# GpSimd's weight sums of the third pair of projection blocks, placed ahead of the wait for the last tokens' rows

## What is computed

```python
def token_mixers(h, p, s_gdn, conv_buf, s_rwkv, h_prev):
    proj = h @ p['w_in']
    qa, ka, va, za, ba, aa, ub, vb = split_cols(proj[..., :C_OFF], AB_SPLITS)
    qkv, new_conv = causal_short_conv(jnp.concatenate([qa, ka, va], axis=-1), conv_buf, p['gdn_conv_w'])
    ...                                   # gated DeltaNet on q, k, v
    u = jax.nn.gelu(ub.astype(f32), approximate=False)
    ...                                   # vs: normalised gelu(vb)
    o_b = u * sgu_mix(vs, p['sgu_w'], p['sgu_b']).reshape(b, L, D_B)
    ...                                   # RWKV-7 on the remaining columns
    mix = jnp.concatenate([o_a, o_b, o_c], axis=-1).astype(h.dtype) @ p['w_out']
    return mix, new_gdn, new_conv, new_rwkv, h[:, -1], vs.reshape(b, L, D_B)
```

## Time and profile before

| | us |
|---|---|
| time before, median of 3 runs | 1267.41 (1266.54 to 1269.93) |
| time of the profiled execution | 1270.75 |
| its span, first to last instruction | 1269.0 |
| TensorE busy | 1188.6 (94% of the span) |
| VectorE busy | 518.8 (41%) |
| ScalarE busy | 339.5 (27%) |
| GpSimd busy | 560.3 (44%) |

### The profile page before, as it was taken

How to read it: one execution, slowest core, us unless ns; L and a number is a source line. 1 busy time by engine, 2 the same in 40 slices (tenths; PEclk the granted TensorE clock), 3 DMA queues, 4 the chain that set the end, 5 groups by cost and what they waited for, 6 DMA issues and landing times. The chain is left out here.

```text
span 1269.0 us, 31522 instructions
## 1 busy us (share of the span) xinstructions
PE 1188.6 (94%) x12736; PEld 849.9 (67%) x12736; DVE 518.8 (41%) x1252; ACT 339.5 (27%) x787; POOL 560.3 (44%) x818
## 2 busy tenths in 40 slices
PE   9996999999999999999998999959999999999990
PEld 7785888856666667778764554447777777777760
DVE  3453887755285524564532113252222222222223
ACT  5002003253342145456432132211111111111114
POOL 7403111020650236878732021026666666666662
PEclk9998999999999999999998999969999999999995
DMA  6301120114303100000084313189999897898838
GB/s 208 100 1 34 35 67 18 32 60 137 63 21 92 50 17 15 17 23 16 11 243 159 101 67 113 45 303 381 308 373 338 270 374 247 289 374 288 266 51 290
DMA packets 139882, 187.12 MB, mean 147 GB/s; under 512 B 37272, under 2 KB 85903, under 8 KB 139786
## 3 DMA queue, kind: packets, MB, share of 16 engines
q1 hardware_dynamic: 123018, 164.87, 38.3%
q0 software_dynamic: 15936, 20.57, 7.8%
q10 hardware_dynamic: 832, 0.33, 0.1%
HBM read 156.41 MB, written 29.32 MB: 146 GB/s over the span
## 5 line engine op out<-in xcount | busy, mean ns | idle before, releaser
L527 PE MATMUL ps<-hT,w_in 128*128 128x352 f32 (+1 forms) x624 | 190.1, 464 | 1.8 <-ACT cb L806 1.2
L527 PEld LDWEIGHTS ps<-hT,w_in 128*128 128x128 f32 x624 | 118.0, 191 | 69.3 <-issue 4.6
L3041 POOL DMA_INDIRECT sum_rows<-slot_out,scatter_rows x76 | 121.9, 1604 | 38.2 <-POOL scatter_rows L3040 25.7
L3173 DVE TENSOR_TENSOR slot_T<-slot_raw_T,vecs 128x256 f32<-128x256 f32 x75 | 32.5, 434 | 208.5 <-PE ps L3086 207.6
L3086 PE MATMUL ps<-qkv,slot_T 128*32 128x256 f32 x1920 | 109.9, 379 | 3.1 <-DVE slot_T L3173 1.6
L3086 PEld LDWEIGHTS ps<-qkv,slot_T 128*32 128x32 f32 x1920 | 74.8, 110 | 32.3 <-DVE slot_T L3173 4.2
L3018 POOL DMA_INDIRECT gathered<-h_rows,gather_rows x79 | 83.5, 1057 | 19.6 <-issue 12.2
L3130 ACT ACTIVATE slot_silu<-ps 128x128 f32<-128x128 f32 x77 | 21.4, 278 | 225.0 <-PE ps L3086 222.8
L3086 PE MATMUL ps<-cb,slot_T 128*32 128x256 f32 x1408 | 80.6, 379 | 0.0
L3086 PEld LDWEIGHTS ps<-cb,slot_T 128*32 128x32 f32 x1408 | 55.4, 110 | 20.5
L3136 ACT ACTIVATE slot_out<-ps,slot_weights 128x256 f32<-128x256 f32 x76 | 36.2, 476 | 112.2 <-PE ps L3097 112.2
(11 more groups left out here) (748 smaller groups left out, 2405.0 us busy)
## 6 DMA issues: line engine op xcount, KB each, us to landing
qkv<-in_expert_w_gate SPq DMA_DIRECT2D x6, 2048.0 KB
qkv<-in_expert_w_up SPq DMA_DIRECT2D x6, 2048.0 KB
qkv<-in_expert_w_down SPq DMA_DIRECT2D x6, 2048.0 KB
cb<-in_expert_w_gate SPq DMA_DIRECT2D x5, 2048.0 KB
cb<-in_expert_w_up SPq DMA_DIRECT2D x5, 2048.0 KB
zg<-in_expert_w_down SPq DMA_DIRECT2D x5, 2048.0 KB, 21.8
third_w_down<-in_expert_w_down SPq DMA_DIRECT2D x5, 2048.0 KB, 17.0
w_in<-in_w_in SPq DMA_DIRECT2D x18, 512.0 KB, 4.7
```

Source lines behind the costliest of these rows:

```text
L527: last = pe.matmul(pbank(b)[:, c, 0:n], w[:, k, :], hT[:, k, c * CH:c * CH + n], start=(k == 0), stop=(k == KD - 1))
L3041: pool.indirect_dma_start(quarter_sums, bass.IndirectOffsetOnAxis(ap=sidx[:, r:r + 1], axis=0), y[r][:], None, compute_op=ALU.add).then_in ...
L3173: dve.tensor_tensor(xT[:], xr[:], bc(nf, 2, ROWS_SLOT), ALU.mult).then_inc(s.xT, 1)
```

## The change

The call `weight_sums(2)` moves up by three statements, from behind the two row DMAs to ahead of the wait for `s.shc`. Nothing else changes; each instruction, its operands and its waits are the same.

```diff
                 pool.wait_ge(s.samp_w, 16 * NB * H)
                 pool.tensor_tensor(m.sguS[:], m.sguS[:], bc(m.causal4[:], 1, H), ALU.mult).then_inc(s.consts, 1)
+                weight_sums(2)
                 pool.wait_ge(s.shc, 2)
                 pool.dma_start(O["shift_prompt"].rearrange("o b d -> (o b) d"), last_rows[0:1, :]).then_inc(s.shift_out, 16)
                 pool.dma_start(O["shift_sample"].rearrange("o b d -> (o b) d"), last_rows[1:1 + NB, :]).then_inc(s.shift_out, 16)
-                weight_sums(2)
                 weight_sums(3)
                 pool.wait_ge(s.vn, 3)
```

## The result

| | before | after |
|---|---|---|
| time, median | 1269.93 us (7 runs, 1266.54 to 1274.96) | 1258.74 us (7 runs, 1256.67 to 1259.33) |
| ratio to before | | 0.9908, 95% interval 0.9892 to 0.9925 |
| profiled execution, its span | 1270.75, 1269.0 us | 1259.14, 1257.4 us |

The change makes the kernel 11.2 us faster by the medians, and 0.92% faster (11.7 us) by the ratio, with 0.75 to 1.08% (9.5 to 13.7 us) as its interval. Forecast were 12.7 us and a time of 1254.7. The time came out 4.0 us above the forecast and 0.2 us above the range's upper end: 2.5 us of that is that the kernel before has a median of 1269.93 over seven runs, where the three runs that the forecast started from gave 1267.41; 1.5 us is gain that did not come.

What follows compares the result with a forecast made beforehand. An order, not work, bounds the stretch: TensorE waits for sums queued behind row DMAs. Idle 10.11 plus clock 2.58, overlap 0, gives 12.69 us; 1267.41 − 12.69 = 1254.7 us, range 1251.0 to 1258.5.

Steps and rivals of the forecast that it cites:

- What bounds the kernel: After the last transposes TensorE idles 10.11 us for GpSimd's sums, queued behind row DMAs they do not need.
- When the sums can run: Third pair's sums start at about 82.0 us, after the first pair's last product, and end between 87.1 and 89.7.
- What TensorE gets back: At the third pair: 10.11 us of idle time plus 2.58 us of clock, together 12.69 us.
- the clock's share: The third pair's first two products, slow after the rest, return to full clock: 2.58 us.
- The fourth pair's sums in time: Ready between 118 and 128 us, wanted by TensorE at 135.4: at least 7 us of cover.
- The overlap: Fourth pair's sums beside VectorE's first convolution delay it 3.0 to 5.1 us; slack 3.7, path cost 0 to 1.4, taken as 0.
- Rival A: Overlap costs 1.4 us at the product behind L1093, as much again with fifth pair's sums; 1256.1 to 1257.5 us; chance 0.13.
- The port rule: VectorE and GpSimd take turns at shared ports, the later blocked for a whole instruction; gain could drop to 11.3 us.
- The sum and the range: Whole kernel: 1267.41 less 12.69 gives 1254.7 us; range for 8 in 10 is 1251.0 to 1258.5.
- B: Behind 250 us, some wait set by something that did not move gives the gain back; up to 1267.4 us; chance 0.04.
- C: Third pair's weights land late, so the moved sums wait and the change does nothing; 1267.4 us; chance 0.01.
- D: Without its rest at 108 us TensorE falls to half clock inside products; slower, 1273.7 us for one fall; chance 0.02.

Runs made afterwards that it cites:

- wait_then_sums: The changed kernel with the wait for the last tokens' rows again ahead of the third pair's sums, row DMAs still behind them; 1267.13 us, ratio 0.9986 to before.
- sums_twice: The changed kernel with GpSimd computing the fourth pair's four weight sums twice; 1260.30 us, ratio 0.9932 to the kernel before.
- filler_5us: The changed kernel with 22 unneeded matmuls (5.0 us) on TensorE behind the last transposes; 1262.93 us, ratio 0.9941 to the kernel before.
- gate_first: The changed kernel with VectorE doing the second batch's gate ahead of the first two adds of the fourth pair's second half; 1257.43 us, ratio 0.9904 to before.
- before_warm_short: The kernel before with 42 unneeded matmuls on TensorE behind the last transposes, where it waits for the sums; 1266.07 us, ratio 0.9976 to before.

## Why the prediction was right, and where it was off

- **What bounds the kernel.** Right. The stretch was bound by an order, and removing the order closed it. wait_then_sums parts it: 9.4 us on the wait, 3.4 on the two DMAs and the gap.
- **When the sums can run.** Right: 83.21 us, with this execution's shift of 1.03 that is 82.2 against the 82.0 forecast. They end at 88.5, 20 us ahead of TensorE.
- **What TensorE gets back.** Right, 12.69 forecast and 12.80 measured; the clock's share of 2.58 was measured by itself at 2.55.
- **The fourth pair's sums in time.** Right: done at 122.0, wanted at 136.3.
- **The overlap.** The mechanism and its size were right: VectorE's convolution took 3.6 us more, inside the bounds of 3.0 and 5.1, and the product behind L1093 just escaped (the add ends at 125.24, TensorE needs it at 125.35). Wrong was the step from there to a cost of 0. The prediction checked the two places where TensorE needs a bank from VectorE, and held them to be the tightest. TensorE needs a third thing of VectorE in this stage, the end of the second batch's gate (L1078) for its last mix, and there the slack was not 3.7 but 0.4 us: before the change the multiply ends at 174.20 + 0.69 = 174.89 and the mix starts at 175.27.

  VectorE in the kernel before, and TensorE's mix:

```profile
174.20 0.69 DVE L1078 TENSOR_TENSOR ub<-ub,cb 128x512 f32<-128x512 f32 x1
```

```profile
175.27 0.42 PE L604 MATMUL ps<-sgu_wT_sample,cb 32*64 32x32 f32 x8
```

  Of VectorE's delay 1.0 us was still left there in the changed kernel (the gate ends 55.19 us from the transposes, where 67.03 less 12.80 would be 54.23), so 0.6 us of waiting, and 1.2 in the second profile. This is the gate's last multiply there:

```profile
163.39 0.69 DVE L1078 TENSOR_TENSOR ub<-ub,cb 128x512 f32<-128x512 f32 x1
```

  How 1.0 us was left can be followed on VectorE. It lost 3.6 us at the first convolution and 0.9 more at the first batch's gate, whose two multiplies took 1.26 and 1.01 us in place of 0.69 beside the fifth pair's sums. It won 3.0 back at the convolution that those sums had held up before the change (154.37 to 163.04) and that now runs alone, and the rest in 0.6 us of idle time that it no longer has. So the change moved an overlap as well as adding one, which the prediction's sum does not have: it let VectorE get nothing back.

  Rival A had this mechanism and its price of 1.4 to 2.8 us, but at the product behind L1093 and too dear; sums_twice makes that form of it come, filler_5us takes the cause away, and gate_first takes the effect away.
- **The port rule.** The Trainium skill, page SBUF — State Buffer, section "Who interferes with whom", says which VectorE instructions contend with GpSimd: those with two SBUF inputs, against a GpSimd instruction that reads SBUF, and copies and scalar operations in a two-port mode. Whichever engine issues first keeps the shared ports for the whole instruction. This case's trace agrees in kind: VectorE's adds, which read one operand from a bank and one from SBUF, kept their 0.43 us beside the sums, while the two-input steps of the convolution went from 0.25 to 1.25 us and from 1.28 to 2.37, and GpSimd's sums from 1.27 to 2.24. The full price of four sums, 5.1 us, was not reached: 3.6 in the changed kernel.
- **The sum and the range.** The gain was 11.2 us by medians, 11.7 by the ratio (9.5 to 13.7), for 12.7 forecast. The last mix stands 12.1 us ahead in the first profile of the changed kernel and 11.4 in the second, and the term taken as 0, the overlap, is what they lack to 12.8. The absolute forecast started from a median of three runs that lay 2.5 us below that of seven. The prediction allowed three microseconds for such a shift; together with the missing gain it came to 4.0 and left the range of 1251.0 to 1258.5 by 0.2. That the gain of the medians came so near the forecast is in part luck, since the interval of the gain is wider than the miss.
- **Rivals B, C and D** did not come; a part of B smaller than the scatter of the later work (3.7 us, below) can't be excluded. D had the clock fall in uninterrupted work: from the third pair into the fourth it stays at 1.00, as this view of the changed kernel by stretch shows, with columns as in the earlier trace rows.

```profile
108.40:118.60 10.20, 10.20 (x49) 8.63 (x49) 4.99 (x10) 1.67 (x2) 4.36 (x5) 1.00 0.42 108
118.60:124.80 6.20, 6.20 (x30) 5.29 (x29) 5.97 (x6) 0.04 (x1) 3.21 (x2) 1.00 0.00 0
124.80:146.00 21.20, 21.20 (x119) 17.70 (x118) 19.05 (x35) 2.79 (x4) 5.81 (x5) 1.00 0.20 52
```

**What was not the change.** The transposes start 1.03 us later in the first two profiles of the changed kernel. The loss lies between TensorE's products at 36 us and the first pair: from the first product behind the 0.6 us wait there (L527) to the last transposes it is 71.70 us before and 73.39 after. Less the 0.66 us by which that product started earlier, this is the 1.03. It is not the change's: before_warm_short, which has the old order, takes 73.24, and sums_twice, filler_5us and gate_first, which have the new one, take 71.70, 71.70 and 71.69. Of the ten profiles five are short and five long. The clock tells them apart: two stretches that begin 0.1 us ahead of that product, the first of the changed kernel, the second of filler_5us. The five long profiles have 0.63 to 0.65 there, the five short ones 1.00.

```profile
35.40:40.00 4.60, 4.50 (x10) 2.71 (x11) 4.55 (x2) 0.00 (x0) 0.00 (x0) 0.63 0.85 225
```

```profile
36.50:41.00 4.50, 4.38 (x15) 2.93 (x16) 4.43 (x2) 0.00 (x0) 0.00 (x0) 1.00 0.89 225
```

From the first normalisation product to the first expert product the ten profiles take 589.5 to 593.2 us, the kernel before being near the top with 593.0. That is a spread of 3.7 us for like work, so the -13.88 in the table of landmarks is no gain of the change. What sets this spread was not pursued.

## What to carry to other kernels

An engine that issues outputs and also makes operands for another engine should not make the operands behind a wait for the outputs: look in front of every long idle time of the matrix engine for what the releasing engine was itself waiting for, and whether the released work needs it. Add to the idle time what the clock takes after it, which the first rows behind the wait show (2.6 us here). And when work is moved beside another engine's, list everything that the critical engine takes from that other engine, not only the busiest hand-over, with the slack of each: the smallest slack decides, and it may sit two stages on.

## What the runs showed of the hardware

- A wait of TensorE of 1.91 us in mid-work (sums_twice) took the granted clock to 0.59 over the next 4.2 us and cost another 1.8 us. Waits of 0.6 and 1.2 us at the last mix did not: the products behind them started 1.9 and 1.8 us apart, as in the kernel before.
- What the clock took did not grow with the wait, in one profile each: 0.1 us behind a wait of 0.68 us (before_warm_short), 1.8 behind 1.91, 2.9 behind 6.34 (wait_then_sums) and 2.6 behind 10.11 (before).
- Five of ten profiles, whatever the kernel, lose 1.5 to 1.7 us to the clock between 35 and 40 us, behind a wait of 0.6 us that all of them have.
- The gap of 2.5 to 2.6 us behind GpSimd's first sum after two DMA issues, present in all three profiles with the old order, was 0.49 us where the DMAs came right behind other sums (wait_then_sums). What it hangs on stays open; only that it is no fixed price of the DMAs is shown.
